# Key and value pages issued by two engines, the state matrices in the weight ring, and the key mask two samples later

## The reference

```python
ki_past = cache_kidx[l, page_table].reshape(B, past, IDX_DIM)
idx, valid = select_keys(qi, w, ki_all, pos, jnp.arange(L, dtype=jnp.int32), topk)   # topk = 256
kg = jnp.where(in_past, cache_k[l, phys, off].astype(k.dtype), gather_rows(k, nidx))
vg = jnp.where(in_past, cache_v[l, phys, off].astype(v.dtype), gather_rows(v, nidx))
return attend_selected(q, kg, vg, valid)
```

```python
C_new = decay[..., None, None] * C + jnp.einsum('bhs,bhsv,bhsd->bhvd', wk, vb, kb)
```

## Time and profile before

| | |
|---|---|
| median of 3 runs | 2297.4 us (2294.43 to 2304.3) |
| the profiled execution, its own time | 2290.72 us |
| its span in the trace | 2289.0 us |
| TensorE busy | 2006.0 us (88%), granted clock 0.907 on average |
| VectorE, ScalarE, GpSimd busy | 48%, 19%, 13% |
| DMA | 174.28 MB, 76 GB/s over the span, 24.1% of 16 engines |
| issues of pages by SP | 256 of 128 KB and 128 of 32 KB |

### The profile page before, as it was taken

How to read it: one execution, slowest core, us unless ns; L and a number is a source line. 1 busy time by engine, 2 the same in 40 slices (tenths; PEclk the granted TensorE clock), 3 DMA queues, 4 the chain that set the end, 5 groups by cost and what they waited for, 6 DMA issues and landing times. The chain is left out here.

```text
span 2289.0 us, 30947 instructions
## 1 busy us (share of the span) xinstructions
PE 2006.0 (88%) x11890; PEld 1625.5 (71%) x11890; DVE 1097.8 (48%) x1992; ACT 441.3 (19%) x966; POOL 301.5 (13%) x280
## 2 busy tenths in 40 slices
PE   5999999687398999999969999978855989999998
PEld 4765566454157999999957656755522679999998
DVE  3375985673003433345425669757710053333553
ACT  2123233223101000021021323341311010000400
POOL 2453430210000000000025424102100000000000
PEclk8899998678698999999959999986787999999999
DMA  3220300313512222213123212012235112323131
GB/s 113 100 90 10 112 1 1 113 42 116 182 37 74 74 74 94 91 53 100 52 62 115 74 31 91 1 42 72 70 118 188 37 37 84 102 74 100 52 102 65
DMA packets 194284, 174.28 MB, mean 76 GB/s; under 512 B 30946, under 2 KB 173570, under 8 KB 193618
## 3 DMA queue, kind: packets, MB, share of 16 engines
q1 hardware_dynamic: 194130, 172.23, 24.1%
HBM read 158.03 MB, written 14.17 MB: 75 GB/s over the span
## 5 line engine op out<-in xcount | busy, mean ns | idle before, releaser
L1075 PE MATMUL psum<-x_high,w_split_even 128*128 128x272 f32 x1408 | 247.6, 294 | 14.7 <-DVE x_low L1881 14.7
L1075 PE MATMUL psum<-x_high,w_split_odd 128*128 128x272 f32 x1408 | 236.8, 288 | 0.0
L1075 PEld LDWEIGHTS psum<-x_high,w_split_even 128*128 128x128 f32 x1408 | 206.1, 193 | 19.4 <-issue 19.4
L1056 PE MATMUL psum<-h_high,w_split_even 128*128 128x272 f32 x1232 | 204.5, 287 | 1.7 <-issue 1.7
L1075 PEld LDWEIGHTS psum<-x_high,w_split_odd 128*128 128x128 f32 x1408 | 199.5, 188 | 0.0
L1906 DVE TENSOR_TENSOR proj<-rawr,psum 128x544 f32<-128x544 f32 x44 | 31.7, 721 | 333.1 <-PE psum L1075 333.1
L1056 PEld LDWEIGHTS psum<-h_high,w_split_even 128*128 128x128 f32 x1232 | 173.4, 188 | 2.5 <-issue 2.5
L1009 PE MATMUL psum<-h_high,x_high 128*128 128x512 f32 (+1 forms) x400 | 168.0, 420 | 1.5 <-ACT proj L794 1.5
L1009 PE MATMUL psum<-h_high,x_low 128*128 128x512 f32 (+1 forms) x400 | 162.0, 405 | 0.0
L1009 PE MATMUL psum<-ring_low,x_high 128*128 128x512 f32 (+1 forms) x400 | 160.9, 402 | 0.0
L630 POOL TENSOR_TENSOR ring_low<-ring,h_high 128x512 fp32r<-128x512 f32 (+1 forms) x96 | 158.5, 1651 | 7.7
(11 more groups left out here) (360 smaller groups left out, 3452.7 us busy)
## 6 DMA issues: line engine op xcount, KB each, us to landing
ring<-in_w_gate_up_dram SPq DMA_DIRECT2D x44, 1024.0 KB, 7.4
ring<-in_w_in_dram SPq DMA_DIRECT2D x14, 2048.0 KB, 8.2
ring<-in_w_down_dram SPq DMA_DIRECT2D x16, 1408.0 KB, 7.0
ring<-in_w_out_dram SPq DMA_DIRECT2D x4, 2048.0 KB, 8.4
ring<-in_cache_k_dram SPq DMA_DIRECT2D x48, 128.0 KB, 2.0
cq<-in_cache_k_dram SPq DMA_DIRECT2D x48, 128.0 KB, 2.0
x_spill<-x SPq DMA_DIRECT2D x2, 2176.0 KB, 14.2
x<-x_spill SPq DMA_DIRECT2D x2, 2176.0 KB, 8.8
```

Source lines behind the costliest of these rows:

```text
L1056: mm = pe.matmul(out[:, 512 * hf:512 * hf + HALF], down_part(c, w)[:, cols], v[:, HALF * hf:HALF * hf + HALF], start=(k == 0 and q == 0), ...
L1075: mm = pe.matmul(out[:, 512 * hf:512 * hf + HALF], w_part(f, w)[:, k, u, :], v[:, k, HALF * hf:HALF * hf + HALF], start=(k == 0 and q == 0 ...
```

## The change

1. **Value pages** of samples 0, 5, 2, 3, 4, 6, 7 are issued by GpSimd, behind its last work of the layer, with its own reads of the page table (`load_values`). SP keeps all key pages and the values of sample 1.
2. **The states** `c0` lie in the first half of `ring` instead of `cq`. They are loaded after the fourth tile of the convolution (`CONV0 + 4`) instead of after the last (`OUT0`). The keys of samples 0 and 1 go into `cq`, those of 2 and 3 into the first half of `ring`.
3. **The mask**: `PICKS_TURN` goes from 6 to 2 and `PICKS_MEM` from 8 places to 4, so 14 rounds instead of 6 stand after the turning; group 0 is closed after the logits of sample 5 instead of 3, and its exponentials follow the copies of all keys.
4. **The loop over the samples** on PE becomes one loop over 8; the first probabilities are turned before the logits of sample 7.
5. **The layer's end**: GpSimd resets its DMA queue and clears the eight semaphores of the value pages itself.

```diff
-PICKS_CONV, PICKS_TURN, PICKS_MEM = 12, 6, range(1, 16, 2)
+PICKS_CONV, PICKS_TURN, PICKS_MEM = 12, 2, range(3, 16, 4)
-        c0 = cq[:, 0:4096].rearrange("p (b h d) -> p b h d", b=DB, h=MH)
+        c0 = ring[:, 0:4096].rearrange("p (b h d) -> p b h d", b=DB, h=MH)
-        K_PLACE = (first0, first1, cq0, cq1, spare0, qk0, cq0, first0)
+        K_PLACE = (cq0, cq1, first0, first1, spare0, qk0, cq0, first0)
...
-                sp.wait_ge(s_out_done, OUT0)
+                sp.wait_ge(s_out_done, CONV0 + 4)
                 for b in range(DB):
                     sp.dma_start(c0[:, b, :, :], A["state_C"][lay, b, :, :, :].rearrange("a h v d -> v (a h) d")).then_inc(s_c0_in, 16)
+                sp.wait_ge(s_out_done, OUT0)
                 sp.dma_start(nrow, A["state_n"][lay, :, :, :].rearrange("a b h d -> (a b) (h d)")).then_inc(s_c0_in, 16)
...
+                load_keys(0)
+                load_keys(1)
+                for g in range(PAGES):
+                    sp.dma_start(v_pages(1)[:, g, :], A["cache_v"][page(PAGES + g), :, :].rearrange("a p d -> p (a d)")).then_inc(v_in[1], 16)
+                load_keys(5)
                 sp.wait_ge(s_tail_copied, 1)
...
-                load_pages(0, ("cache_k",))
-                load_pages(1, ("cache_k", "cache_v"))
-                load_pages(5, ("cache_k",))
                 sp.wait_ge(s_c_new, MH)
...
-                load_pages(2, ("cache_k",))
-                load_pages(3, ("cache_k",))
+                load_keys(2)
+                load_keys(3)
                 sp.wait_ge(s_a_turned, 4)
-                load_pages(4, ("cache_k",))
-                load_pages(0, ("cache_v",))
-                load_pages(2, ("cache_v",))
-                load_pages(3, ("cache_v",))
-                load_pages(4, ("cache_v",))
-                load_pages(5, ("cache_v",))
+                load_keys(4)
                 sp.wait_ge(s_kt_turned, 4)
-                load_pages(7, ("cache_k",))
-                sp.wait_ge(s_kt_turned, 4 * 4)
-                load_both(6)
+                load_keys(6)
+                sp.wait_ge(s_kt_turned, 4 * 3)
+                load_keys(7)
                 sp.wait_ge(s_x_spilled, 16)
                 sp.dma_start(x[:, :], x_spill).then_inc(s_x_back, 16)
-                sp.wait_ge(s_kt_turned, 4 * 5)
-                load_pages(7, ("cache_v",))
...
+                def load_values(b):
+
+                    for g in range(PAGES):
+                        row = pool.value_load(pages[0:1, b * PAGES + g:b * PAGES + g + 1], min_val=0, max_val=POOL - 1)
+                        pool.dma_start(v_pages(b)[:, g, :], A["cache_v"][bass.ds(l * POOL + row, 1), :, :].rearrange("a p d -> p (a d)")).then_inc(v_in[b], 16)
+
+                pool.wait_ge(s_num, MH)
+                load_values(0)
+                pool.wait_ge(s_c_sum, 1)
+                load_values(5)
+                pool.wait_ge(s_stored, 16 * STORES)
+                load_values(2)
+                load_values(3)
+                pool.wait_ge(s_a_turned, 4)
+                pool.wait_ge(s_s_turned, 1)
+                load_values(4)
+                pool.wait_ge(s_kt_turned, 4 * 2)
+                load_values(6)
+                pool.wait_ge(s_kt_turned, 4 * 5)
+                load_values(7)
...
-                    if b == 6:
-                        pe.wait_ge(s_s_ptc, 1)
...
-                    pe.wait_ge(s_kt_copied, 24 if g == 0 else 32)
+                    pe.wait_ge(s_kt_copied, 4 * DB)
...
-                for b in range(5):
-                    turn_keys(b + 1)
+                for b in range(DB):
+                    if b + 1 < DB:
+                        turn_keys(b + 1)
+                    if b == DB - 1:
+                        turn_probs(0)
                     sample_logits(b)
-                    if b == 3:
+                    if b == 5:
                         finish_logits(0)
-                turn_probs(0)
-                sample_logits(5)
-                turn_keys(6)
-                turn_keys(7)
-                sample_logits(6)
-                sample_logits(7)
+                pe.wait_ge(s_s_ptc, 1)
                 finish_logits(1)
...
+            nc.gpsimd.dma_reset()
+            for s in v_in:
+                nc.gpsimd.sem_clear(s)
+            for i, s in enumerate(s for s in layer_semaphores if s not in v_in):
```

More of the change, by code:

```diff
@@ L535, in _, with load_keys @@
                 sp.dma_start(O["m_s"][lay, :, :].rearrange("a b h -> h (a b)"), mrow[:, 1:9], allow_slow_non_contiguous=True).then_inc(s_kv_stored, 16)
-                sp.wait_ge(s_out_done, OUT0)
+                sp.wait_ge(s_out_done, CONV0 + 4)
                 for b in range(DB):
                     sp.dma_start(c0[:, b, :, :], A["state_C"][lay, b, :, :, :].rearrange("a h v d -> v (a h) d")).then_inc(s_c0_in, 16)
+                sp.wait_ge(s_out_done, OUT0)
                 sp.dma_start(nrow, A["state_n"][lay, :, :, :].rearrange("a b h d -> (a b) (h d)")).then_inc(s_c0_in, 16)
-                def load_pages(b, names):
+                def load_keys(b):
                     for g in range(PAGES):
-                        at = page(b * PAGES + g)
-                        for name in names:
-                            buf, sem = (k_pages(b), k_in[b]) if name == "cache_k" else (v_pages(b), v_in[b])
-                            sp.dma_start(buf[:, g, :], A[name][at, :, :].rearrange("a p d -> p (a d)")).then_inc(sem, 16)
-                def load_both(b):
-                    load_pages(b, ("cache_k", "cache_v"))
+                        sp.dma_start(k_pages(b)[:, g, :], A["cache_k"][page(b * PAGES + g), :, :].rearrange("a p d -> p (a d)")).then_inc(k_in[b], 16)
+                load_keys(0)
[3 more added lines that the diff above has]
+                load_keys(5)
                 sp.wait_ge(s_tail_copied, 1)
@@ L961, in sample_probs @@
                     act.activation(s_pt[g][0:NS, 8, :], ps(2)[0:NS, P:2 * P], ACT.Copy).then_inc(s_s_ptc, 1)
-                for b in range(6):
-                    copy_keys(b)
-                sample_probs(0)
+                copy_keys(0)
+                copy_keys(1)
+                copy_keys(2)
+                copy_keys(3)
+                copy_keys(4)
+                copy_keys(5)
                 copy_keys(6)
                 copy_keys(7)
+                sample_probs(0)
                 sample_probs(1)
```

1 line of the change is left out of this document (removed).

## The result

The changed kernel takes 2190.4 us (median of 4 runs, 2182.2 to 2205.8) where the kernel before takes 2295.9 us (4 runs): a ratio of 0.9539, 95% interval 0.949 to 0.9588. The prediction said 2190, from 2165 to 2255. TensorE is busy for 2008.3 us, as before, now 92% of the span. The profiled execution took 2193.1 us with a span of 2191.5, so the span is 97.5 us shorter than before; the prediction had 107.6.

A forecast was written before the change was run, and what follows sets the result against it. SP's page issuing, 1.10 us each, was taken to end TensorE's 46.3 us key wait. Per layer 46.0 + 8.6 + 1.2 - 2.0 = 53.8 us, 107.6 for two, gave 2190 us, range 2165 to 2255.

The forecast's parts named there:

- the row: Key-page wait: trace showed 1.10 us per issue and DMA engines 0.44 busy, so a second issuer removes the wait.
- the bound of 1.10: Value pages on GpSimd: lower bound per issue, taken from SP's 1.10 us a page; upper bound 3.1 us.
- the limit of 1.88: Value pages on GpSimd: up to 1.88 us a page no stall; each 0.1 us above costs 5.6 us a layer.
- one page at a time: Rival: GpSimd issues a page only when the one before has landed, 3.1 us each, 2327 us; chance 0.08.
- A hold-up by VectorE: Rival: GpSimd issues pages only in VectorE's gaps, the last landing 30 us late, 2251 us; chance 0.05.
- All three arrive with 0.9 us or more to spare: Sample attention: keys of samples 4, 6 and 7 land before TensorE asks; the wait gone, 46.0 us a layer.
- The rival of late keys: Key pages arrive late beside value pages in flight, 4 to 10 us a layer from sample 4, 2205 us; chance 0.05.
- The sum of 9.8 us: Memory stage, per layer: 8.6 us from an earlier start of the decays, 1.2 us from rounds removed in the heads.
- TensorE's part then ends at 430.5: Memory stage, first part: TensorE ends at 430.5 instead of 433.3, and the decays start 8.6 us sooner.
- Behind the others DVE then waits for TensorE: Memory heads: of four rounds removed, one gains 1.2 us; at the others VectorE waits for TensorE anyway, gaining nothing.
- the seven rows: Layer's end: seven more GpSimd rows between the barriers cost 2 us a layer, bounds 0 and 7.6.
- its 2183: Forecast for the profiled execution: 2290.7 us less 107.6 for two layers; the median was put 6.7 higher, at 2190.

The follow-up runs named there:

- (1): The kernel before with only the issue of the 56 value pages a layer moved to GpSimd, key pages in old order on SP: 2204.2 us, ratio 0.9588.
- (2): The changed kernel with the 56 value pages issued by SP again, behind all key pages, and the layer's end of before: 2238.3 us, ratio 0.9701.
- (3): The changed kernel with each GpSimd value page issued as two halves, each with its own table read, 112 issues a layer: 2250.0 us, ratio 0.9749.
- (4): The changed kernel with 24 unused VectorE copies between SBUF tiles ahead of the 14 mask rounds, beside GpSimd's value pages: 2231.7 us, one run.
- Run 5: The changed kernel with the value pages of samples 0 and 5 issued after the end of the state stores instead of ahead of it: 2183.4 us, one run.
- (8): The changed kernel run and traced once more without any edit (the second trace): 2193.7 us, ratio 0.9489 to the kernel before.

## Why the prediction was right, and where it was not

- **The cause of the wait: right, and shown.** Moving the issues (1), putting them in another order on one queue (2) and doubling their number (3) move the time as a count of issues times 1.10 or 1.15 us says. Against the rule of the Trainium skill, "DMA: Bandwidth & Descriptors", section "Issuing engines are not separate DMA queues" (a second issuer saves only a start that is usually small), the runs decide for the row: the starts of 56 pages are 64 us of a layer, and moving them saved 45.1.
- **GpSimd's price: right.** 1.15 us a page beside the bound of 1.10 that was taken; the limit of 1.88 was borne out by 3. Of the rivals, one page at a time is seen nowhere, since pages 1.15 us apart land after 3.0. A hold-up by VectorE costs nothing: GpSimd goes on at 1.15 us beside 14 rounds without a break, and the hold-up that copies do cause fits into its pause (4).
- **The sample attention: right in kind, 2.6 us too high.** The step that failed is "All three arrive with 0.9 us or more to spare": TensorE waits 1.1 to 2.9 us for the keys of sample 4. The sum had kept two terms of the kernel before. The landing is 2.8 us beside value pages, not 2.0; and SP, behind stores that take 2 us longer, starts on the keys 5.4 us ahead of the first turned keys, not 7.0. The rival of late keys was there, at 2.6 us where it had 4 to 10, and with half of its reason. Run 5 gives the lead back, keeps the landing of 2.8, and gets the full 46 us (54.9 against 100.9).
- **The memory stage: right total, wrong parts.** The sum of 9.8 us met 8.3. The earlier first state is right (2.8, measured 2.6). "TensorE's part then ends at 430.5" failed: it ended at 436.6, since the part took 28.6 us at a granted clock of 0.50. The heads gave this back: they took 52 to 54.5 us instead of 62.4, where the forecast had 1.2 us. Here "Behind the others DVE then waits for TensorE" and its "nothing" failed. In layer 0, 6.9 us of the gain lie ahead of the first head's values (439.13 to 468.33, are 29.2 us; 436.70 to 459.02 are 22.3), where three rounds stood and one stands now; 2.0 lie between the first head and the second. The other reason may again be the clock, 0.82 from 456 to 491 us where the earlier trace rows have a mean of 0.67; no run keeps rounds and clock apart. The prediction had put the clock aside as a gain of up to 8 us; in the runs it is a scatter of up to 10 us a layer with either sign (73.3 to 83.2 us from the first state to the heads' end, over twelve layers with the same code there).
- **The layer's end: too dear, and made up for elsewhere.** The turn took 0.5 us more, not 2 (0.7 in the second trace); the kernel of 2, which has the layer's end of before, takes 8.1 us too, so not even that is shown to be the seven rows'. Most of the 2.3 us that the rest of the layer lost are TensorE's: the first 96 products of the output projection took 23.9 to 24.0 us in all four layers instead of 22.27, at a lower granted clock (0.96 in the window 608.5 to 650).
- **The exact hit of the median is luck within that.** The profiled execution missed its 2183 by 10 us; single executions of this kernel lie up to 24 us apart.

## What to carry to other kernels

When an engine waits for transfers and the DMA engines are not busy, count the issues in the queue ahead of the late one and multiply by the price of one; then first put them in the order in which they are needed, and then split them over two issuers. Look also at what an issue is made of: where two pages share one read of the table the second costs less than half (below). A second issuer's pages lengthen the landing of the first one's and the stores that they go out beside, so keep them away from those that have only a microsecond to spare. Do not book a gain that rests on one trace's clock level: trace the kernel twice first.

## What the hardware showed that was not expected

- GpSimd's pages came 1.2 to 2.3 us apart while 2 MB of states were being stored, and 1.15 us apart when issued after the stores (5), with VectorE idle during part of the slow ones (495.3 to 499.4 us). What in the stores slows them is open.
- Half a page of 64 KB costs the same 1.15 us to issue as a whole one of 128 KB (3), each with its own read of the table.
- Most of an issue's price on SP is the read of the table. The kernel before issues the keys and values of sample 6 from one read, and the second page follows 0.44 us after the first, a pair each 1.57 us instead of twice 1.10:

```profile
596.09 0.33 SPq L548 DMA_DIRECT2D cq<-in_cache_k_dram  x1
596.53 0.38 SPq L548 DMA_DIRECT2D cq<-in_cache_v_dram  x1
597.66 0.33 SPq L548 DMA_DIRECT2D cq<-in_cache_k_dram  x1
```

  Whether pairs alone would have ended the wait, no run here tried.
- An issue row of GpSimd beside a VectorE copy between SBUF tiles ends 0.12 us after the copy's end where it would have ended during it (4).
- TensorE, busy 28.59 of 29 us with no wait, was granted 0.50 throughout, that is 1.2 GHz; the same instructions in other layers and executions rose to 2.4 GHz after their start and took 19.3 us. The pause ahead of them was the same 6.3 us; what goes with the two courses is when in the pause the clock fell (8). Why, is open.
